# Gate-row buffers, down-projection waits, table order and a written-out TensorE loop in an expert stage

## The reference, cut to what matters

```
def _moe(h, router, w_gate_up, w_down):
    logits = h @ router
    top_v, top_i = lax.top_k(logits, 2)
    gates = softmax(top_v)                      # two gates per token
    y = 0
    for e in range(8):
        g, u = split(h @ w_gate_up[e])          # 1024 -> 2 x 3584
        y += gate_full[:, e:e+1] * ((silu(g) * u) @ w_down[e])   # 3584 -> 1024
```

## Time and profile before

| | us |
|---|---|
| median of 3 runs (1622.4 to 1627.42) | 1624.27 |
| the profiled execution | 1621.72 |
| its span, first to last instruction | 1619.8 |
| TensorE busy (93% of the span) | 1507.9 |
| DVE busy (73%) | 1175.7 |
| ACT busy (62%) | 1003.5 |
| GpSimd busy (9%) | 137.8 |

### The profile page before, as it was taken

How to read it: one execution, slowest core, us unless ns; L and a number is a source line. 1 busy time by engine, 2 the same in 40 slices (tenths; PEclk the granted TensorE clock), 3 DMA queues, 4 the chain that set the end, 5 groups by cost and what they waited for, 6 DMA issues and landing times.

```text
span 1619.8 us, 20671 instructions
## 1 busy us (share of the span) xinstructions
PE 1507.9 (93%) x7570; PEld 1219.2 (75%) x7570; DVE 1175.7 (73%) x1008; ACT 1003.5 (62%) x861; POOL 137.8 (9%) x130
## 2 busy tenths in 40 slices
PE   8999999999999989899889998889999889999885
PEld 6888888899789967677767786666887666787763
DVE  5554554465655558798879887879897879888886
ACT  5444343343543367567778776778776868777774
POOL 0000000040304034000001000001000001000000
PEclk9999999999999999999999999999999999999998
DMA  9655555557356525999999999999999999999993
GB/s 337 203 182 182 182 181 183 182 183 234 105 154 211 184 73 185 347 325 365 388 384 365 387 384 330 373 366 372 383 388 336 387 364 370 383 386 363 389 386 114
DMA packets 238180, 469.58 MB, mean 290 GB/s; under 512 B 9792, under 2 KB 15936, under 8 KB 238064
## 3 DMA queue, kind: packets, MB, share of 16 engines
q1 hardware_dynamic: 231504, 453.93, 79.2%
q0 software_dynamic: 3072, 11.01, 2.3%
q10 hardware_dynamic: 3488, 3.13, 0.6%
HBM read 460.67 MB, written 7.37 MB: 289 GB/s over the span
## 4 chain that ended last, share of the span: by engine, by line
PE 74%; DVE 11%; ACT 7%; issue 7%; DMA 1%; SPq 0%; DVEq 0%; ACTq 0%
DVE wlo L318 8%; ACT whi L312 6%; PE bY L335 6%; PE bY L337 5%; PE bY L336 5%; PE bG L335 5%; PE bG L337 5%; PE bG L336 5%; PE bU L335 5%; PE bU L337 5%; PE bU L336 5%; PE bS L337 3%; PE bS L336 3%; PE bS L335 3%; PE bT L884 3%
## 5 line engine op out<-in xcount | busy, mean ns | idle before, releaser
L318 DVE TENSOR_TENSOR wlo<-raw,whi 128x2048 fp32r<-128x2048 f32 x426 | 971.4, 2299 | 351.9 <-ACT whi L312 350.8
L312 ACT ACTIVATE whi<-raw 128x2048 fp32r<-128x2048 f32 x426 | 811.6, 1914 | 415.4 <-PE bS L337 132.9
L871 PE MATMUL bG<-whi,eTh 128*128 128x512 f32 x224 | 96.6, 431 | 40.7 <-DVE wlo L318 34.1
L871 PE MATMUL bY<-whi,hTh 128*128 128x512 f32 x224 | 95.5, 427 | 21.9 <-DVE hTh L1320 15.8
L871 PEld LDWEIGHTS bG<-whi,eTh 128*128 128x128 f32 x224 | 43.7, 195 | 70.8 <-DVE wlo L318 46.0
L335 PE MATMUL bG<-whi,eTh 128*128 128x512 f32 x224 | 90.5, 404 | 5.9 <-DVE eTl L1320 3.8
L871 PE MATMUL bU<-whi,eTh 128*128 128x512 f32 x224 | 91.6, 409 | 3.1 <-DVE wlo L318 2.9
L335 PE MATMUL bU<-whi,eTh 128*128 128x512 f32 x224 | 92.2, 411 | 0.0
L872 PE MATMUL bY<-wlo,hTh 128*128 128x512 f32 x224 | 91.7, 409 | 0.0
L872 PE MATMUL bG<-wlo,eTh 128*128 128x512 f32 x224 | 91.5, 408 | 0.0
L335 PE MATMUL bY<-whi,hTh 128*128 128x512 f32 x224 | 89.7, 401 | 1.0 <-DVE hTl L1320 1.0
(11 more groups left out here) (436 smaller groups left out, 2941.4 us busy)
## 6 DMA issues: line engine op xcount, KB each, us to landing
raw<-in_m_w_gate_up_dram SPq DMA_DIRECT2D x224, 1024.0 KB, 9.6
raw<-in_m_w_down_dram SPq DMA_DIRECT2D x112, 1024.0 KB, 7.8
raw<-in_b_w_in_dram SPq DMA_DIRECT2D x36, 1024.0 KB, 5.2
raw<-in_f_w_gate_up_dram SPq DMA_DIRECT2D x28, 1024.0 KB, 5.3
raw<-in_f_w_down_dram SPq DMA_DIRECT2D x14, 1024.0 KB, 5.1
raw<-in_a_w_out_dram SPq DMA_DIRECT2D x4, 1024.0 KB, 15.1
biasrev<-toeplitz SPq DMA_DIRECT2D x32, 128.0 KB, 5.1
raw<-in_b_w_out_dram SPq DMA_DIRECT2D x4, 1024.0 KB, 5.2
```

What stands on the lines that cost most here:

```text
L312: nc.scalar.activation(whi[:, t % CUT], raw[:, t % RAW], ACT.Copy).then_inc(hi_done, 1)
L318: nc.vector.tensor_tensor(wlo[:, t % CUT], raw[:, t % RAW], whi[:, t % CUT].bitcast(F32), ALU.subtract).then_inc(lo_done, 1)
L871: pe.matmul(backward(bank, 0, 512), xs[:, kb], w[0], start=kb == 0, stop=False)
```

## The change

1. A second gate row, `gate_odd`, is placed; slabs take the two in turn (`gate_rows(j)`). ACT's copy of slab j waits for the fold matmuls of slab j-2 instead of j-1, and turn_slab reads the row of its slab.
2. In the down-projections of both kinds of item TensorE waits ahead of each tile of the first output half for the low part of just the slab that this tile needs. In full items the wait that protects bank T stands between the first down tile and the turn.
3. The pieces of the routing tables move: experts_by_load joins gates_by_expert in slab 0, every later piece stands one slab earlier, and the four overflow pieces are spread over slabs 4, 5 and 6.
4. TensorE's loop over items 1 to 6 is a Python loop, so its instructions are written out with constant counts. The loops of SP, ACT and DVE stay.

```diff
@@ -206,6 +206,8 @@
         y_out = place("y_out", [D], F32)
         e_tok = place("e_tok", [D], F32)
         top[0] = at_xT
+        gate_odd = place("gate_odd", [512], F32)
+        gate_rows = lambda j: (mbuf[:, 0], gate_odd[:])[j % 2]
         tsilu = place("tsilu", [256], F32)
         th = place("th", [256], F32)
         fold = place("fold", [HALF_CAP], F32)
@@ -851,12 +853,11 @@
                     product(4 * j + 3, eTh, eTl, KH[1], U, True)
                 for h in range(2):
                     for qn, ks in enumerate(down):
+                        if h == 0:
+                            pe.wait_ge(ht_lo, count(k, SLABS, PAIRS0 + qn + 1))
+                        product(DOWN + DT * h + qn, hTh, hTl, ks, (Y0, Y1)[h], qn == DT - 1)
                         if h == 0 and qn == 0:
                             pe.wait_ge(ht_lo, count(k, SLABS, PAIRS0 + SLABS - 1))
-                        if h == 0 and qn == DT - 1:
-                            pe.wait_ge(ht_lo, count(k, SLABS, PAIRS0 + SLABS))
-                        product(DOWN + DT * h + qn, hTh, hTl, ks, (Y0, Y1)[h], qn == DT - 1)
-                        if h == 0 and qn == 0:
                             turn_hidden(SLABS - 1, 1, lambda tb: mh, count(k, SLABS, PAIRS0 + SLABS))
                         if h == 1 and qn == 3:
                             late()
@@ -878,7 +879,7 @@
                     pe.wait_ge(up_copied, count(k, SLABS, j + 1))
                     if j >= 1:
                         pe.wait_ge(jt_mul, count(k, SLABS, j))
-                    for part, src in enumerate((msilu, mh)):
+                    for part, src in enumerate((gate_rows(j), mh)):
                         for c in range(4):
                             to = slice(part * 256 + c * HALF_CAP, part * 256 + (c + 1) * HALF_CAP)
                             mm = pe.matmul(T[:, to], src[:, c * P:c * P + P], fold[:], start=True, stop=True)
@@ -901,10 +902,8 @@
                     product(4 * j + 3, eTh, KH[1], U, True)
                 for h in range(2):
                     for qn, ks in enumerate(down):
-                        if h == 0 and qn == 0:
-                            pe.wait_ge(jt_lo, count(k, SLABS, SLABS - 1))
-                        if h == 0 and qn == DT - 1:
-                            pe.wait_ge(jt_lo, count(k, SLABS, SLABS))
+                        if h == 0:
+                            pe.wait_ge(jt_lo, count(k, SLABS, qn + 1))
                         product(DOWN + DT * h + qn, hTh, ks, (Y0, Y1)[h], qn == DT - 1)
                         if h == 0 and qn == 0:
                             turn_slab(SLABS - 1)
@@ -929,9 +928,9 @@
 
             full_item(0, 0, first_amid, lambda: turn_tokens(0))
             pe.wait_ge(fold_ready, 1)
-            with pe.Fori(0, LOW - 1) as r:
-                half_item((r, 2, 1), (r, 1, 0), **ahead_of((r, 2, 1)))
-                full_item((r, 2, 2), (r, 1, 1), **ahead_of((r, 2, 2)))
+            for r in range(LOW - 1):
+                half_item(2 * r + 1, r, **ahead_of(2 * r + 1))
+                full_item(2 * r + 2, r + 1, **ahead_of(2 * r + 2))
 
             def last_amid(j):
                 if j == 1:
@@ -1225,9 +1224,9 @@
                 for j in range(SLABS):
                     ahead(4 * j)
                     act.wait_ge(tile_used, count(n, FFN_TILES, T_MOE + 4 * j + 2))
-                    if j >= 1:
-                        act.wait_ge(jt_psum, count(k, SLABS, j))
-                    copy(msilu, G[:], gate_copied)
+                    if j >= 2:
+                        act.wait_ge(jt_psum, count(k, SLABS, j - 1))
+                    copy(gate_rows(j), G[:], gate_copied)
                     if j >= 1:
                         slab_silu(j - 1)
                     ahead(4 * j + 1)
@@ -1767,8 +1766,8 @@
                     if t == DOWN + DT + 4:
                         late()
 
-            aside = {0: gates_by_expert, 1: experts_by_load, 2: tables_by_slot, 3: table_of_rows,
-                     4: full_experts, 5: lambda: [overflow(0), overflow(1)], 6: lambda: [overflow(2), overflow(3)]}
+            aside = {0: lambda: [gates_by_expert(), experts_by_load()], 1: tables_by_slot, 2: table_of_rows,
+                     3: full_experts, 4: lambda: overflow(0), 5: lambda: [overflow(1), overflow(2)], 6: lambda: overflow(3)}
             full_item(0, 0, **routed(0, 48, True), aside=aside)
             with dve.Fori(0, LOW - 1) as r:
                 half_item((r, 2, 1), (r, 1, 0), **routed((r, 2, 1), count((r, 1, 0), 48, 64), False))
```

## The result

| | median us | runs | ratio to before |
|---|---|---|---|
| kernel before | 1623.83 | 4 (1622.4 to 1627.42) | 1 |
| changed kernel | 1599.1 | 4 (1598.18 to 1600.4) | 0.9845 [0.9827, 0.9863] |

The change saves 24.7 us.

What follows compares the result with a forecast made beforehand. TensorE bounds full items, the weight chain half items, with the DMA nearly full. 11.8 + 16.4 + 5.1 + 0 = 33.3 us, less 7 returned by the DMA, 26.3 off: 1598 us, own range 1590 to 1605, overall 1585 to 1611.

Steps and rivals of the forecast that it cites:

- Part 1, the ring: Half-item slabs: a second gate row shortens the slab's chain of waits by 0.49 us in 24 slabs, 11.8 us.
- Part 2, the down-projection: Start of half items' down-projections: waits by slab remove TensorE's hTh wait, 4.1 us in each of four, 16.4 us.
- Part 3, the tables: Item 0: table wait goes, 6.1 us, less 1.8 in slab 0, plus 0.8 from later slabs; net 5.1 us.
- Part 4, the loop: Two back edges: TensorE's 2.8 us dry lies beside ACT's stalls, so 0 us; bounds -1.5 to 5.8 each.
- What the DMA gives back: Weight loads: 1 us returned each in items 1, 3, 5 and 4 in the last; 7, between 2 and 14.
- the prediction's own room: Items 1, 3, 5: free DMA 2.2 to 3.4 us plus next item's margin 2.2, 4.4 to 5.6 of 7.0.
- the full item's lower demand helps: Full items behind items 1, 3, 5: lower DMA demand, counted toward only 1 us returned each.
- The margins: Weight loads: lead over landings (10.3 us in the median, up to 13.5) leaves 2 to 3 us.
- rival B: DMA is the real wall: half items keep only 2.2 us each, 13.9 us remain, 1610 us; chance 0.18.
- A: Back edges come free too with TensorE's loop written out: 8 us more at best, 1590 us; chance 0.12.
- C: TensorE's straight code stalls on fetches, 1692 us; mark: new idle time with "issue" as the reason; chance 0.03.
- D: Change does not do what it says: ACT's copy still late, or clock drops elsewhere; 1620 us; chance 0.05.

Runs made afterwards that it cites:

- loop_only: Kernel before with only TensorE's loop over items 1 to 6 written out: 1624.29 us, 0.9993.
- after_loop_back: Changed kernel with TensorE's loop put back, the other three parts kept: 1598.31 us, 0.9843.
- before_half_bytes: Kernel before with half of each expert weight tile left out of its load from item 1 on: 1619.72 us, 0.9966.
- after_half_bytes: Changed kernel with half of each expert weight tile left out of its load from item 1 on: 1578.4 us, 0.9712.
- after_all_out: Changed kernel with the loops of ACT, DVE and SP over items 1 to 6 written out too: 1588.82 us, 0.9776.
- after_act_out: Changed kernel with ACT's loop over items 1 to 6 written out too: 1596.87 us, 0.9827.

## Why the prediction was right, and where it was not

- **Part 1, the ring.** Right: ACT's copy no longer waits, slabs at 10.67 us, DVE next with 1.10 us of slack. 11.8 forecast, 13.4 alone.
- **Part 2, the down-projection.** Right: no wait for hTh, clock 1.00, 3.6 to 4.2 us an item for 4.1. Alone 18.0 for 16.4; what a gap costs differs between executions with the clock after it.
- **Part 3, the tables.** Right in the net: 5.1 forecast, 5.4 alone, 5.5 in the trace. In the profiled execution its price was 3.2 for 1.8, since the clock fell after the wait; in most others it was 1.9, so 1.8 was a sound figure and this execution an unlucky one. The give-back of the later slabs was too low (1.6 for 0.8).
- **Part 4, the loop.** Right: 0, since ACT's stall ends later; shown from both sides by loop_only and after_loop_back, to within some 2 and 5 us, and by the first slabs, 16.0 to 16.4 us with and without. Not seen: SP's stall at the same place, because the prediction followed only who made TensorE late, and not who made the loads late.
- **What the DMA gives back.** This is the term that was mis-sized: 7 us forecast (bounds 2 and 14), 10.3 measured where ACT waits for landings, 12.8 with the clock behind the back edges. It was 1 us each in items 1, 3 and 5, and is 1.7, 1.4 and 1.3 (1.7, 2.7 and 2.5 with the clock); it was 4 in the last item, and is 5.9. By the prediction's own room (4.4 to 5.6 of 7.0) 1.4 to 2.6 would go back; the three items stand at the near end of that, without the credit that "the full item's lower demand helps", which made it 1. That credit had little ground in the rows: outside SP's stall the DMA was hardly ever free in item 2 of the kernel before (share 1.05 over its first 100 us), so most of what the 1.01 of its window in the earlier trace rows leaves is SP's stall, and no room for an earlier half item. And the clock behind a back edge had no term in the DMA's sum at all. The margins used the landings of before, a median of 10.3 us; at saturation they move too. SP's loads of the changed kernel from 845 to 865 us, at the end of item 1, and from 1480 to 1520 us:

```profile
DMA to landing us min/median/max: 13.2/14.2/15.2
...
DMA to landing us min/median/max: 14.0/14.3/14.4
```

  With 14.2 us to a landing and 11.1 to 14.4 us of lead, ACT waits. Waits on landings in item 1, which the prediction gave as a mark of rival B, did come (3.2 us between 835 and 863), and the full items behind them lost nothing (+0.2, -1.2, +0.1), as the forecast said.
- **The sum.** The parts alone gave 37.3 for 33.3 (+4.0), their combination lost 12.6 for 7 (-5.6). The errors nearly cancel: 24.7 for 26.3. That 1599.1 lies 1.1 us from the forecast is partly luck; the terms were good to 4 to 6 us, which is also what their measurement can tell.
- **The rivals.** A fell: the back edges stayed. B held in one item of four: the last keeps 1.2 us of its 7, while items 1, 3 and 5 keep 4.3 to 5.5 where B gave 2.2. C fell, though its mark came: the weight loads show "issue" 28 times (33.2 us, in the waits above), once a slab, and 8 times (7.7 us) with the loop put back. But the kernel is no faster then (after_loop_back), and slabs take 10.67 us either way, so this costs nothing that can be measured. D fell.

## What to carry to other kernels

At a loop's end look at every engine's sequencer, the one that issues the loads first of all: here unrolling paid in full only when the last of them was unrolled. Near a transfer limit gains don't add up (37 us of parts gave 25), and the room left is to be worked out with the landing times of a full queue, not those of today's. Cutting the bytes and nothing else separates what the engines gained from what the transfers take back.

## What was not expected of the hardware

**A branch's stall depends on the traffic.** With all bytes ACT's is 5.4 us. With half of them, in before_half_bytes and after_half_bytes:

```profile
L1257 ACTq COMPARE_BRANCH  x1: 58/58/58, 1000.4 to 1000.4; - x1
L1257 ACTq FUSED_REGOPS  x1: 50/50/50, 1003.7 to 1003.7; - x1
```

```profile
L1256 ACTq COMPARE_BRANCH  x1: 58/58/58, 983.4 to 983.4; - x1
L1256 ACTq FUSED_REGOPS  x1: 50/50/50, 986.5 to 986.5; - x1
```

3.3 and 3.1 us. In before_half_bytes SP's is 4.2 us for 5.4 and TensorE's branch 5.0 for 6.67. So on three engines the stall is 1.2 to 2.3 us shorter with half of the bytes (DMA share 0.64).

**Two paces of TensorE at one granted clock.** In a full item, where TensorE is never idle, two windows of the kernel before in one execution (the earlier trace rows has 900:950 with x221):

```profile
1140.00:1190.00 50.00, 50.00 (x225) 40.20 (x224) 44.85 (x33) 36.52 (x26) 0.00 (x0) 1.00 1.05 387
```

221 or 225 matmuls in 50 us, both at 1.00. Their starts are 0.240 or 0.233 us apart; a slab of a full item takes 11.95 or 11.64 us. The slow pace is seen in slabs alone: every down-projection of a full item from item 2 on takes 36.72 us in this trace, at 0.233. It can begin in the middle of an item (item 4 of after_all_out) and stands in other items in other kernels, so it isn't tied to the change. It makes up to 1.6 us an item: much of the +-1 us of items 2, 4 and 6 in the table above. What sets it is open.

**Also open**: SP's and DVE's loops were not written out apart from each other. The traces point to SP for the 8 us between after_act_out and after_all_out: DVE's sequencer goes on 0.35 us after its branch (1000.45 to 1000.80 in before), and in after_act_out its wlo follow each other without a gap there.
